# Layer norms with a 128-column root, four-lane openings and the mean read from PSUM, in a two-block kernel on one core

## What is computed

```python
def layer_norm(x, g, b):
    xf = x.astype(jnp.float32)
    mu = jnp.mean(xf, axis=-1, keepdims=True)
    var = jnp.mean(jnp.square(xf - mu), axis=-1, keepdims=True)
    return ((xf - mu) * lax.rsqrt(var + LN_EPS) * g + b).astype(x.dtype)

for l in range(DEPTH):                       # DEPTH = 2
    mix = token_mixing(x, w_in[l], ...)      # attention and others, ends in @ w_o
    x = layer_norm(ALPHA * x + mix, ln1_g[l], ln1_b[l])
    ff = conv_ffn(x, ffn_w_up[l], ...)       # starts with x @ w_up
    x = layer_norm(ALPHA * x + ff, ln2_g[l], ln2_b[l])
```

## Time and profile before

| what | us |
|---|---|
| median of 3 runs | 3851.48 (3850.53 to 3851.8) |
| the profiled execution's own time | 3853.62 |
| span of the profile of that execution | 3851.4 |
| TensorE busy | 3666.2 (95%) |
| VectorE / ScalarE / GpSimd busy | 1701.6 / 1496.9 / 1272.5 |

### The profile page before, as it was taken

How to read it: one execution, slowest core, us unless ns; L and a number is a source line. 1 busy time by engine, 2 the same in 40 slices (tenths; PEclk the granted TensorE clock), 3 DMA queues, 4 the chain that set the end, 5 groups by cost and what they waited for, 6 DMA issues and landing times.

```text
span 3851.4 us, 47530 instructions
## 1 busy us (share of the span) xinstructions
PE 3666.2 (95%) x17456; PEld 2877.5 (75%) x17456; DVE 1701.6 (44%) x2436; ACT 1496.9 (39%) x2440; POOL 1272.5 (33%) x584
## 2 busy tenths in 40 slices
PE   8999998999899999989998998999999999999997
PEld 7777786888687777868886676788744588777886
DVE  2444447443334534664325643603247554526042
ACT  3246633332322665243325544423224143444232
POOL 4322133444343112434443143444200011433443
PEclk9999999999999999999999999999999999999999
DMA  3321122223223111222232232222322200322222
GB/s 136 104 67 49 44 72 76 96 95 104 86 93 104 44 44 49 94 77 98 98 99 88 95 102 66 88 94 97 105 82 74 69 1 1 110 71 82 98 94 81
DMA packets 100352, 310.92 MB, mean 81 GB/s; under 512 B 25952, under 2 KB 26080, under 8 KB 99552
## 3 DMA queue, kind: packets, MB, share of 16 engines
q1 hardware_dynamic: 81792, 298.90, 23.3%
q10 hardware_dynamic: 18400, 9.78, 0.9%
HBM read 302.35 MB, written 5.24 MB: 80 GB/s over the span
## 4 chain that ended last, share of the span: by engine, by line
issue 51%; PE 28%; POOL 18%; DVE 1%; ACT 0%; POOLq 0%; DVEq 0%; DMA 0%; SPq 0%
POOL ring_r L2695 18%; PE ps L454 6%; PE ps L455 6%; PE ps L456 6%; PE ps L967 2%; PE ps L1067 1%; PE ps L805 1%; PE ps L986 1%; PE ps L1143 0%; PE ps L1112 0%; PE ps L1125 0%; PE ps L1103 0%; PE ps L1135 0%; PE ps L1145 0%; PE ps L1205 0%
## 5 line engine op out<-in xcount | busy, mean ns | idle before, releaser
L2695 POOL TENSOR_TENSOR ring_r<-ring,rounded_r 128x1024 fp32r<-128x1024 f32 x504 | 1234.9, 2453 | 2094.0 <-ACT rounded_r L1248 2093.5
L454 PE MATMUL ps<-source_hi,rounded_r 128*128 128x512 f32 x2560 | 1021.8, 399 | 96.0 <-DVE X_lo L1969 31.3
L1248 ACT ACTIVATE rounded_r<-ring 128x1024 fp32r<-128x1024 f32 x504 | 533.8, 1059 | 1325.3 <-PE ps L456 1209.8
L455 PE MATMUL ps<-source_hi,ring_r 128*128 128x512 f32 x2560 | 1006.4, 393 | 0.0
L454 PEld LDWEIGHTS ps<-source_hi,rounded_r 128*128 128x128 f32 x2560 | 486.8, 190 | 216.4 <-DVE X_lo L1969 33.8
L456 PE MATMUL ps<-X_lo,rounded_r 128*128 128x512 f32 x1536 | 602.5, 392 | 0.0
L455 PEld LDWEIGHTS ps<-source_hi,ring_r 128*128 128x128 f32 x2560 | 487.3, 190 | 102.2 <-issue 3.1
L456 PEld LDWEIGHTS ps<-X_lo,rounded_r 128*128 128x128 f32 x1536 | 291.0, 189 | 62.2
L456 PE MATMUL ps<-N_lo,rounded_r 128*128 128x512 f32 x768 | 302.4, 394 | 0.0
L2238 DVE SCALAR_TENSOR_TENSOR T<-ps,PAR,T 128x511 f32<-128x511 f32 (+1 forms) x176 | 131.5, 749 | 227.8 <-ACT T L1446 211.5
L454 PE MATMUL ps<-H_hi,rounded_r 128*128 128x512 f32 x512 | 199.2, 389 | 0.0
(11 more groups left out here) (502 smaller groups left out, 5609.5 us busy)
## 6 DMA issues: line engine op xcount, KB each, us to landing
ring<-in_weights SPq DMA_DIRECT2D x560, 512.0 KB, 3.3
X<-in_x SPq DMA_DIRECT2D x2, 1024.0 KB, 6.9
out_x<-X SPq DMA_DIRECT2D x4, 512.0 KB, 2.6
SWAP<-Z ACTq DMA_DIRECT2D x4, 256.0 KB, 6.1
MEM<-in_mem ACTq DMA_DIRECT2D x1, 1024.0 KB, 4.8
mem_keys<-Z ACTq DMA_DIRECT2D x1, 1024.0 KB, 3.9
diag_in<-Y ACTq DMA_DIRECT2D x8, 128.0 KB, 2.2
Z<-diag_in ACTq DMA_DIRECT2D x8, 128.0 KB
```

The source lines that it names most:

```text
L454: mm(o, lh, rh, start=start, stop=False)
L455: mm(o, ll, rh, start=False, stop=False)
L1248: av(RH[:, j, :], ring[:, j, :], ACT.Copy).then_inc(w_hi, 1)
L2695: nc.gpsimd.tensor_tensor(RL[:, j, :], ring[:, j, :], RH[:, j, :].bitcast(F32), ALU.subtract).then_inc(w_lo, 1)
```

## The change

- Variance, root and reciprocal work on 128 columns. Mean and mean of squares are alike on all partitions, so partitions 32b to 32b + 31 take token block b: four subtractions of 32x128 fill `QSUM[:, 0:128]`, one root and one reciprocal follow on 128x128.
- TensorE spreads the factor over all partitions again: `spread`, four products of 128x128 with one column of the identity as a broadcast stationary operand, into bank 6. The scaling reads bank 6 instead of `RS`.
- The copy of the mean is gone; the subtractions read bank 4.
- On VectorE the variance comes before the subtraction from tile 0, subtractions run two tiles ahead, and the remainder of tile n comes behind the scaling of tile n + 1 and a subtraction (that of tile 0 before the scaling of tile 1).
- On ScalarE the rounding of slot 3 (`last_slot`) stands right behind the root instead of behind the last tile.
- The openings behind the four norms use four lanes instead of three.

```diff
+            def spread(l, i):
+                pe.wait_ge(ln["dve"], (l * 2 + i) * LN_DVE + LN_ROOT)
+                for b in range(ST):
+                    row = cst("ident")[:, b * 32:b * 32 + 1].to_broadcast([P, P])
+                    ins = mm(ps[:, 6, b * P:b * P + P], row, RS[:, 0:P], start=True, stop=True)
+                ins.then_inc(ln["sums"], 1)
...
-                first_quad(W0, 0, XH, XL, x_ready, l * 16, 2, (zc, l * C_Z), 2 if l == 0 else RING - 1)
+                first_quad(W0, 0, XH, XL, x_ready, l * 16, 2, (zc, l * C_Z), 2 if l == 0 else RING)
...
                 sums_of(l, 0, KT - 1)
-                first_quad(W0 + n_split(B_UP), 0, XH, XL, x1, l * KT, 1, (up_c, l * C_UP))
+                spread(l, 0)
+                first_quad(W0 + n_split(B_UP), 0, XH, XL, x1, l * KT, 1, (up_c, l * C_UP), RING)
...
                 sums_of(l, 1, KT - 1)
+                spread(l, 1)
...
-            gemm(B_LRU, C_LRU_IN, AH, NL, scaled, 0, SRC["lru_in"], 0, 0, third=mem_squares)
+            gemm(B_LRU, C_LRU_IN, AH, NL, scaled, 0, SRC["lru_in"], 0, 0, third=mem_squares, lanes=RING)
...
             def layer_norm(l, i, bias, following):          # ScalarE
-                act.wait_ge(s["sums"], at * 3 + LN_MEAN)
-                av(MEAN, ps[:, 4, :], ACT.Copy).then_inc(s["act"], 1)
+                act.wait_ge(s["sums"], at * LN_SUMS + LN_MEAN)
                 av(SQ[KT % 2], ps[:, 4, :], ACT.Square).then_inc(s["act"], 1)
-                act.wait_ge(s["dve"], at * 3 + LN_VAR)
-                av(RS[:], QSUM, ACT.Sqrt, bias=cst("eps")).then_inc(s["act"], 1)
+                act.wait_ge(s["dve"], at * LN_DVE + LN_VAR)
+                av(RS[:, 0:P], QSUM[:, 0:P], ACT.Sqrt, bias=cst("eps")).then_inc(s["act"], 1)
+                last_slot(following)
...
-                last_slot(following)
...
                 def less(*tiles):                           # VectorE
                     for n in tiles:
-                        tt(X[:, n, :], X[:, n, :], MEAN, ALU.subtract)
+                        tt(X[:, n, :], X[:, n, :], ps[:, 4, :], ALU.subtract)
+                dve.wait_ge(s["act"], at * LN_ACT + LN_MSQ)
+                dve.wait_ge(s["sums"], at * LN_SUMS + LN_SQMEAN)
+                for b in range(ST):
+                    rows, t = slice(b * 32, b * 32 + 32), slice(b * P, b * P + P)
+                    ins = tt(QSUM[rows, 0:P], ps[rows, 5, t], SQ[KT % 2][rows, t], ALU.subtract)
+                ins.then_inc(s["dve"], 1)
                 less(0)
-                dve.wait_ge(s["act"], at * LN_ACT + LN_MSQ)
-                dve.wait_ge(s["sums"], at * 3 + LN_SQMEAN)
-                tt(QSUM, ps[:, 5, :], SQ[KT % 2], ALU.subtract).then_inc(s["dve"], 1)
+                dve.wait_ge(s["act"], at * LN_ACT + LN_STD)
+                v.reciprocal(RS[:, 0:P], RS[:, 0:P]).then_inc(s["dve"], 1)
                 less(1)
-                dve.wait_ge(s["act"], at * LN_ACT + LN_STD)
-                v.reciprocal(RS[:], RS[:])
+                dve.wait_ge(s["sums"], at * LN_SUMS + LN_SPREAD)
                 for t in range(KT + 1):
                     dve.drain()
+                    if t == 1:
+                        low(0)
                     if t < KT:
-                        stt(X[:, t, :], X[:, t, :], par(gain, t, 1), RS[:], ALU.mult, ALU.mult).then_inc(s["y"], 1)
-                    if 2 <= t + 1 < KT:
-                        less(t + 1)
-                    if t >= 1: ... remainder of tile t - 1
+                        stt(X[:, t, :], X[:, t, :], par(gain, t, 1), ps[:, 6, :], ALU.mult, ALU.mult).then_inc(s["y"], 1)
+                    if 2 <= t + 2 < KT:
+                        less(t + 2)
+                    if t >= 2:
+                        low(t - 1)
```

More of the change, by code:

```diff
@@ L305, in build @@
         ln = {k: sem(f"ln_{k}") for k in ("dve", "xc", "qadd", "sums", "act", "y", "hi")}
-        LN_DVE, LN_FIRST, LN_SUM, LN_VAR = 3, 1, 2, 3
-        LN_SHIFT, LN_MEAN, LN_SQMEAN = 1, 2, 3
-        LN_ACT, LN_MCOPY, LN_MSQ, LN_STD = KT + 3, KT + 1, KT + 2, KT + 3
+        LN_DVE, LN_FIRST, LN_SUM, LN_VAR, LN_ROOT = 4, 1, 2, 3, 4
+        LN_SUMS, LN_SHIFT, LN_MEAN, LN_SQMEAN, LN_SPREAD = 4, 1, 2, 3, 4
+        LN_ACT, LN_MSQ, LN_STD = KT + 2, KT + 1, KT + 2
         SQ = [T1[:, 4, :], T1[:, 5, :]]
-        QSUM, SHIFT, MEAN = T1[:, 6, :], T1[:, 7, :], T1[:, 7, :]
+        QSUM, SHIFT = T1[:, 6, :], T1[:, 7, :]
         JUNK = sb("JUNK", [P, 1])
@@ L518, in shift @@
             def shift(l, i):
-                pe.wait_ge(ln["dve"], (l * 2 + i) * 3 + LN_FIRST)
+                pe.wait_ge(ln["dve"], (l * 2 + i) * LN_DVE + LN_FIRST)
                 mm(ps[:, 4, :], cst("mean"), X[:, 0, :], start=True, stop=True).then_inc(ln["sums"], 1)
@@ L806, in mem_keys, with gemm @@
                 ins.then_inc(used, 1)
-            def gemm(first, tiles, hi, lo, free, base, src, bank=0, event=None, before=None, skewed=False, second=None, third=None):
+            def gemm(first, tiles, hi, lo, free, base, src, bank=0, event=None, before=None, skewed=False, second=None, third=None, lanes=RING - 1):
                 done = 0
                 if src is not None:
-                    first_quad(n_split(first), bank, hi, lo, src_lo, src, 1, (free, base), before=before, skewed=skewed)
+                    first_quad(n_split(first), bank, hi, lo, src_lo, src, 1, (free, base), lanes, before, skewed)
                     done = 1
@@ L1943, in less, with low @@
                     for n in tiles:
-                        tt(X[:, n, :], X[:, n, :], MEAN, ALU.subtract)
-                dve.wait_ge(s["act"], at * LN_ACT + LN_MCOPY)
+                        tt(X[:, n, :], X[:, n, :], ps[:, 4, :], ALU.subtract)
+                def low(n):
+                    if at == 2 * DEPTH - 1:
+                        dve.wait_ge(src_hi, HI0 + SRC["lru_in"] + n + 1)
+                        stt(NL[:, n, :], X[:, n, :], par2("ln", n, 1), XHF[:, n, :], ALU.mult, ALU.subtract).then_inc(src_lo, 1)
+                    else:
+                        dve.wait_ge(s["hi"], at * KT + n + 1)
+                        stt(XL[:, n, :], X[:, n, :], par(bias, n, 1), XHF[:, n, :], ALU.add, ALU.subtract).then_inc(done, each)
@@ L1981, in whole_residual @@
                         ins.then_inc(s["dve"], 1)
-                dve.wait_ge(s["sums"], at * 3 + LN_SHIFT)
+                dve.wait_ge(s["sums"], at * LN_SUMS + LN_SHIFT)
                 ts(SHIFT, ps[:, 4, :], float(KT), None, ALU.mult)
```

## The result

| | before | after |
|---|---|---|
| median, us | 3851.80 (3850.53 to 3854.90, 5 runs) | 3869.08 (3866.16 to 3870.80, 5 runs) |
| ratio | | 1.0042 (95% interval 1.0028 to 1.0057) |
| the profiled execution, its own time / its span | 3853.62 / 3851.4 | 3866.16 / 3864.1 |

The change makes the kernel 17 us slower. The direction was forecast, the size (8.6 us) was half of it, and the time lies above the range.

What follows compares the result with a forecast made beforehand. TensorE, busy 95% of the span, was taken as the bound, so only its idle stretches or lowered clock could move the time. Terms +2.2 + 8.4 - 2.0 = +8.6 us gave 3860 us, range 3851 to 3867.

Steps and rivals of the forecast that it cites:

- part 2: Four-lane openings: slot 0 free 4.8 us later from TensorE's start, 7.0 us refill exposed, second quads later, +2.2 us in all.
- Part 3: TensorE's clock: half-clock spells behind the four new gaps, +8.4 us; shorter spells at the openings, -2.0 us.
- Part 1: Shorter chain at the norms, 5.8 us (6.6 at the last): TensorE starts 4.4 us earlier (3.9 at the last), together 17.1.
- The -2.0 us of part 3: Start of the four openings: idle time ahead cut in two, half-clock spell 0.5 us shorter each (bounds 0 and -5).
- Rival 1: Gaps behind the openings: clock falls late or returns soon, and idling ahead lowers it less; +3 us, 3854.5; chance 0.30.
- Rival 2: Behind the openings: refill not exposed, so the earlier starts stay, 17 us faster, 3834; chance 0.06.
- Rival 3: In the norms' chain: GpSimd's slot 3 remainder holds VectorE's first remainder up to 2 us each; +18.6, 3870; chance 0.09.

Runs made afterwards that it cites:

- Both experiments on the lanes: The changed kernel with its four openings put back to three lanes, 3838.15 us; the kernel before with four lanes and slot 3 rounded behind the root, 3882.24 us.
- the gap was filled: The changed kernel with five idle products, read by nobody, on TensorE behind each four-lane opening: 3858.54 us.
- The kernel with the norm kept busy: The changed kernel, four lanes, with idle products on TensorE inside each norm, three ahead of the spread and two behind it: 3859.54 us.

## Why the prediction was right in direction and wrong in size

**The mechanism of part 2 held.** Slot 0 is given back after 87 matmuls instead of 66 (its next transfer is issued 22.3 us behind the start of the opening instead of 17.8 at norm 1), the refill takes 6.8 to 7.0 us against 6.9 to 7.6, TensorE idles 4.9 to 5.1 us at each norm (4.9 forecast). A slip of no weight: 19.2 less 17.1 is 2.1, not 2.2. Both experiments on the lanes came within 3 us of what the same working gave for them.

**Part 3, the spell behind the gap, held.** 8.8 us lost against 8.4 (3.1, 1.5, 2.9 and 1.3, where I had 2.1 for each), and 10.5 us back when the gap was filled.

**Part 1 was mis-sized, by 6.1 us.** The step that failed is the spread: "in attention four such products take 0.68 at full clock; here TensorE has been idle, so I take 0.9". The earlier trace rows says x4, and I took the four records for four products. A full-precision product is two records, as L548 with x8 for four products shows; four products are 1.16 us at full clock and 2.07 to 2.08 at half clock (norms 1 and 3); at norms 4 and 2 the clock fell while they ran, and they took 2.00 and 1.82. The other three norms of the change, then norm 2 of the three-lane kernel, where the same work met full clock:

```profile
1026.78 1.82 PE L548 MATMUL ps<-RS,CST 128*128 128x128 f32 x8 [2.93 <-DVE RS L1971]
1670.57 2.07 PE L548 MATMUL ps<-RS,CST 128*128 128x128 f32 x8 [3.11 <-DVE RS L1971]
2054.39 2.00 PE L548 MATMUL ps<-RS,CST 128*128 128x128 f32 x8 [2.93 <-DVE RS L1971]
...
1018.34 1.16 PE L548 MATMUL ps<-RS,CST 128*128 128x128 f32 x8 [2.93 <-DVE RS L1971]
```

Over the four norms the spread took 8.0 us where I had 3.6: 1.0 of the difference is the count of records, 3.3 the clock. The four variance pieces took 1.19 instead of 0.9, each its full 0.3: small operations one behind the other didn't overlap as I assumed. The chain is 7.36, 7.17, 7.36 and 8.17 us against my 5.8 and 6.6, so the starts came 2.9, 3.0, 2.9 and 2.3 us sooner, 11.0 in all instead of 17.1. Since the refill counts from the start, every microsecond of that came back one for one.

**The -2.0 us of part 3 was wrong.** I expected the two shorter idle stretches around the spread to shorten the half-clock spell of the opening. Over the lengths of the earlier trace rows, counted from TensorE's start, the four openings have 0.91, 0.87, 0.92 and 0.90 against 0.90, 0.91, 0.94 and 0.88 before, and with the spread's share counted the time lost ahead of and in the openings rose from 9.1 to 13.3 us (by the same 2 us stretches). So the spread at half clock cost time and the openings behind it were no faster.

Together 6.1 and 2.8 (the openings without the spread's own 3.4 lost 0.8 more, not 2.0 less), less 1.0 for a refill that was a little shorter (norm 4: 6.8 instead of 7.6): 7.9 of the 8.0 us between 8.6 and 16.6. The kernel with the norm kept busy shows from the other side that the clock is most of it: with the spread at 1.16 us and the opening at full clock, four lanes cost 3859.5 us. That this is my 3860 is luck in part: its four chains are 26.7 us together, still longer than my 24.0, and its openings lose nothing to half clock, where my sum left about 7 there.

**The rivals.** Rival 1, a kinder clock, didn't come: all four second quads were slow, though two of them lost only 1.5 and 1.3 us. Rival 2, a refill that isn't exposed, is what three lanes do, 3838 against its 3834. Rival 3 named +18.6, near the truth, for a wrong reason: GpSimd's remainder of slot 3 ended at 644.80 and the first remainder of VectorE began at 646.35, so nothing was held. That no row shows the lock for the three-operand form, as the prediction says, is not so: the second block of the kernel before has it, in an operation of the remainder's form that takes 0.75 us alone (timeline):

```profile
2249.71 2.40 POOL L2695 TENSOR_TENSOR ring_r<-ring,rounded_r 128x1024 fp32r<-128x1024 f32 x1 [1.92 <-ACT rounded_r L1248]
2250.28 2.38 DVE L2273 SCALAR_TENSOR_TENSOR N_lo<-X,PAR,source_hi 128x512 fp32r<-128x512 f32 x1 [0.57 <-ACT source_hi L1481]
```

It ends 0.55 us after GpSimd's operation, as the 2.45 us subtraction of the earlier trace rows does. So rival 3's mechanism exists, and only its moment didn't come.

**The version that beats both** is the change with three lanes: 3838 us, 14.5 us under the kernel before; with idle products in the norm 3835, 16.5 us under it, which the scatter doesn't part from 14.5.

## What to carry to other kernels

Before more work is moved in front of a buffer's release, ask what lies over the buffer's refill: a whole product behind the opening looked like leftover work, but it was the cover for 7 us of transfer, rounding and remainder, and taking it away cost about 4.5 us and a slow spell at each place. An earlier start is worth only what the next wait leaves of it, so count forward to the second product, not to the first. And before a row is taken as the price of an operation, check how many records one operation makes, and at which clock it will run.

## What the runs showed of the hardware

Four full-precision products of 128 columns take 1.16 us at full clock and 2.08 at half, in eight records; one of 512 columns is two records and 0.86 us (four records of the idle products take 1.88 us, ten take 4.45). The Trainium skill ("FP8 and Floating Point Precision", "TensorE Precision Notes") counts four passes of the array for true FP32. The trace fits that in time, 0.86 us against 0.229 us for one of the rounded matmuls of the same 512 columns, though it shows two records and not four.

VectorE's reciprocal goes by columns, 3.35, 1.74 and 0.95 us for 512, 256 and 128. And it takes the same 3.35 us with GpSimd's remainder beside it, unlike the two operations above that read two SBUF tiles, as this pair from the second block of the kernel before shows (timeline):

```profile
2073.06 2.40 POOL L2695 TENSOR_TENSOR ring_r<-ring,rounded_r 128x1024 fp32r<-128x1024 f32 x1 [0.35 <-ACT rounded_r L1248]
2073.59 3.35 DVE L2256 RECIPROCAL RS<-RS 128x512 f32<-128x512 f32 x1 [12.26 <-ACT RS L1470]
```

One and the same unchanged stretch differs between two executions by where half-clock spells fall: up to norm 1 the profile before takes 634.8 us with 6.8 lost to half clock, the one after 639.8 with 10.8, and behind the fourth second product the eleven profiles lie between 1774.8 and 1785.5 us. That is why two profiles of this kernel are compared norm by norm and not by their spans.
